# Two column halves for both token tiles of the output projection, with the router's first logits moved into the last block

## The reference, cut to what matters

```
for l in range(DEPTH):
    mix = hybrid_mixer(x, ...)                 # ends in  merged @ w_out
    h = layer_norm(DEEPNORM_ALPHA * x + mix, ln1_g[l], ln1_b[l])
    ffn = hierarchical_moe(h, ...)             # best group of 4, best 2 of its 8 experts
    x = layer_norm(DEEPNORM_ALPHA * h + ffn, ln2_g[l], ln2_b[l])
```

## Time and profile before

| | |
|---|---|
| median of 3 runs | 1603.16 us (1602.19 to 1604.07) |
| the profiled execution, own time | 1602.01 us |
| its span, first to last instruction | 1599.4 us |
| busy: TensorE, VectorE, ScalarE | 81%, 39%, 25% of the span |
| mean granted TensorE clock | 0.903 |
| read from HBM | 522.53 MB, 327 GB/s over the span |

### The profile page before, as it was taken

How to read it: one execution, slowest core, us unless ns; L and a number is a source line. 1 busy time by engine, 2 the same in 40 slices (tenths; PEclk the granted TensorE clock), 3 DMA queues, 4 the chain that set the end, 5 groups by cost and what they waited for, 6 DMA issues and landing times. The chain is left out here.

```text
span 1599.4 us, 21372 instructions
## 1 busy us (share of the span) xinstructions
PE 1298.2 (81%) x8678; PEld 878.4 (55%) x8678; DVE 620.5 (39%) x1063; ACT 393.1 (25%) x453; POOL 0.2 (0%) x4
## 2 busy tenths in 40 slices
PE   9999999999756656657799999999997556656666
PEld 7998889995312212212398988899943212212211
DVE  5788676655100100100287876765641000000102
ACT  4334734323100000001143357343320000000010
POOL 0000000000000000000000000000000000000000
PEclk9999999999978877878999999999999778778778
DMA  8455445689999999999964454376999999999996
GB/s 304 162 194 191 165 158 214 245 356 419 426 428 428 428 427 429 427 427 429 404 223 162 159 211 176 115 257 221 408 420 428 426 426 427 430 426 429 427 425 263
DMA packets 98886, 524.58 MB, mean 328 GB/s; under 512 B 5488, under 2 KB 9968, under 8 KB 70144
## 3 DMA queue, kind: packets, MB, share of 16 engines
q1 hardware_dynamic: 98064, 523.10, 81.2%
q10 hardware_dynamic: 752, 0.50, 0.1%
HBM read 522.53 MB, written 1.05 MB: 327 GB/s over the span
## 5 line engine op out<-in xcount | busy, mean ns | idle before, releaser
L1035 PE MATMUL psum<-ring,aqT 128*32 128x512 f32 x1504 | 269.5, 704 | 112.9 <-PEq L1023 112.9
L1723 DVE TENSOR_TENSOR w_low<-ring,w_high 128x2048 fp32r<-128x2048 f32 (+2 forms) x108 | 239.8, 2260 | 72.3 <-DVEq L1722 71.0
L1281 ACT ACTIVATE w_high<-ring 128x2048 fp32r<-128x2048 f32 (+2 forms) x108 | 198.7, 1887 | 193.3 <-ACTq L1277 178.8
L1035 PE MATMUL psum<-spare,aqT 128*32 128x512 f32 x256 | 130.9, 700 | 94.7 <-PEq L1124 94.7
L1959 DVE TENSOR_TENSOR qk<-psum,qk 128x512 f32<-128x512 f32 x16 | 11.1, 692 | 482.5 <-DVEq L1958 482.5
L1035 PEld LDWEIGHTS psum<-ring,aqT 128*32 128x32 f32 x1504 | 68.6, 127 | 218.1 <-issue 218.1
L1035 PE MATMUL psum<-rv,tmp 128*32 128x512 f32 x240 | 124.2, 707 | 70.0 <-PEq L1151 70.0
L712 PE MATMUL psum<-x_high,w_high 128*128 128x256 f32 x512 | 146.8, 287 | 0.0
L712 PE MATMUL psum<-x_high,w_low 128*128 128x256 f32 x512 | 143.3, 280 | 0.0
L712 PE MATMUL psum<-x_low,w_high 128*128 128x256 f32 x512 | 143.2, 280 | 0.0
L619 PE MATMUL psum<-w_high,x_high 128*128 128x512 f32 (+2 forms) x352 | 138.6, 394 | 0.0
(11 more groups left out here) (266 smaller groups left out, 2280.4 us busy)
## 6 DMA issues: line engine op xcount, KB each, us to landing
ring<-in_w_gate_dram SPq DMA_DIRECT2D x56, 2048.0 KB, 33.0
ring<-in_w_in_dram SPq DMA_DIRECT2D x34, 2048.0 KB, 7.8
ring<-in_w_up_dram SPq DMA_DIRECT2D x28, 2048.0 KB, 21.9
spare<-in_w_up_dram SPq DMA_DIRECT2D x14, 2048.0 KB, 14.2
rv<-in_w_down_dram SPq DMA_DIRECT2D x12, 2048.0 KB, 31.0
rg<-in_w_down_dram SPq DMA_DIRECT2D x12, 2048.0 KB, 35.4
x_xT<-in_w_down_dram SPq DMA_DIRECT2D x12, 2048.0 KB, 39.8
ring<-in_w_down_dram SPq DMA_DIRECT2D x12, 2048.0 KB, 28.9
```

Source lines behind the costliest of these rows:

```text
L1035: mm = nc.tensor.matmul(bank[s, :], lhs[:, c, s], w[:, k, n * NB:(n + 1) * NB], start=(c == 0), stop=(c == chunks - 1))
L1281: nc.scalar.activation(half_tile(high, i % HIGH, w, b), half_tile(ring, i % RAW, w, b), ACT.Copy).then_inc(high_ready, 1)
L1723: V.tensor_tensor(half_tile(low, i % RAW, w, b), half_tile(ring, i % RAW, w, b), half_tile(high, i % HIGH, w, b).bitcast(f32), ALU.subtrac ...
```

## The change

The order of TensorE's work in `out_and_logits` and of VectorE's beside it is changed. The numbers of matmuls, transposes and vector instructions stay the same. The second halves of the sum now run (0,0), (1,0), (0,1), (1,1) left, (1,1) right. The 8 transposes and 8 logits of tile 0 move from the middle of block (1, 0) and ahead of (1,1) left into (1,1) right. VectorE adds up block (1, 0) ahead of (0, 1), and `choose(0)` becomes one piece, ahead of the last `add_up`.

```
                 finish("OUT0", out_block(first[:, 0, :], 0, 0, halves[1], began=out_used[0, 1]))
+                finish("OUT1", out_block(second[:, 0, :], 1, 0, halves[1]))
                 pe.wait_ge(low_ready, 1).then_inc(low_ready, -1)
-                finish("OUT0", out_block(first[:, 1, :], 0, 1, halves[1]))
-                out_block(second[:, 0, :], 1, 0, halves[1][:6])
-
-                pe.wait_ge(y_ready, 2)
+                finish("OUT0", out_block(first[:, 1, :], 0, 1, halves[1], began=out_used[1, 0]))
+                finish("OUT1", out_block(last_left, 1, 1, halves[1], left))
+
+                pe.wait_ge(y_ready, 3)
                 turn_sums(0, range(4), ps[:, 0, :])
                 finish("HT0", turn_sums(0, range(4, KC), first[:, 0, :]))
-                finish("OUT1", out_block(second[:, 0, :], 1, 0, halves[1][6:]))
-
+                out_block(last_right, 1, 1, halves[1][:6], right)
                 rl = begin("RL")
                 copied("HT0", "RL")
-                logits(0, range(KC), rl, began=out_used[1, 0])
-                finish("OUT1", out_block(last_left, 1, 1, halves[1], left))
-
-                out_block(last_right, 1, 1, halves[1][:6], right)
+                logits(0, range(KC), rl)
                 ps = begin("HT1")
-                pe.wait_ge(y_ready, 3)
                 finish("HT1", turn_sums(1, range(4), ps[:, 0, :]))
                 finish("OUT0", out_block(last_right, 1, 1, halves[1][6:], right))
```

```
-                for n in range(2):
-                    c = slice(n * NB, (n + 1) * NB)
-                    add_up(0, c, "OUT0", first[:, n, :])
-                    statistics(0, n, c)
+                add_up(0, slice(0, NB), "OUT0", first[:, 0, :])
+                statistics(0, 0, slice(0, NB))
+                add_up(1, slice(0, NB), "OUT1", second[:, 0, :])
+                statistics(1, 0, quarter[0])
+                statistics(1, 1, quarter[1])
+                add_up(0, slice(NB, 2 * NB), "OUT0", first[:, 1, :])
+                statistics(0, 1, slice(NB, 2 * NB))
...
                 V.tensor_scalar(nmx[:, 2:3], mv[:, 0, 0:1], -1.0, rstd[:, 0:1], ALU.mult, ALU.mult
                                 ).then_inc(norm_ready, 1)
-                add_up(1, slice(0, NB), "OUT1", second[:, 0, :])
-                choose(0, group_found=lambda: statistics(1, 0, quarter[0]),
-                       masked_out=lambda: statistics(1, 1, quarter[1]),
-                       expert_found=lambda: add_up(1, quarter[2], "OUT1",
-                                                   second[:, 1, 0:NB // 2]))
+                add_up(1, quarter[2], "OUT1", second[:, 1, 0:NB // 2])
                 free("OUT1")
                 statistics(1, 2, quarter[2])
+                choose(0)
                 add_up(1, quarter[3], "OUT0", banks("HT0")[:, 1, 0:NB // 2])
```

## The result

The changed kernel takes 1608.67 us (median of 16 runs, 1604.18 to 1612.79), the kernel before 1603.16 (16 runs, 1600.78 to 1604.07). The ratio is 1.0035, 95% interval 1.0029 to 1.0042: **slower by 5.6 us**. The forecast was 3.4 us slower, at most 4.4 by its range. Direction and place were right, the size was not. The profiled execution has 1609.78 us of its own time, 7.8 over the profiled one of before, and a span of 1608.0, 8.6 over it (outside the span lie 1.8 us, before 2.6).

A forecast was written before the change was run, and what follows sets the result against it. The streaming of expert weights bounds the kernel, its queue dry at used(1). A last add_up 1.73 us late costs 1.7 us a layer, 3.4 over two layers, giving 1606.6 us, range 1604.3 to 1607.6.

The forecast's parts named there:

- the place and the mechanism: At used(1) the queue of weight loads is already dry, so a later issue costs its full delay, 1.7 us a layer.
- the term that was summed: Last add_up 1.73 us late, 0.60 from TensorE and 1.13 from its place in VectorE's list; 1.7 us a layer.
- the clock falls: Rival: new TensorE pauses among short matmuls halve the granted clock, 3 us a layer more, in sum +9.4; chance 0.05.
- the 16.11 us of work behind the last add_up: Chain from the last add_up through statistics, choose(1), gather and first gate product to used(1)'s issue, taken as unchanged.
- the second pause: TensorE's wait for sel_ready, from 363.6 to 364.7 us, about 1.1 us.
- nothing in the chain to used(1) has slack, so the 16.11 us stay: From the last add_up to used(1): the delay passes through whole, so used(1) is issued at 380.76 us.
- each later load call finds more queued: After used(1) the queue fills; used(1) alone adds 4 MiB, about 10 us, so the pause there decides.
- The queue hides part: Rival at used(1): loads start quicker behind running transfers, 0.92 us of cover, 0.8 a layer, +1.6; chance 0.22.
- the 0.6 us of first-byte latency: At used(1), by the skill's figure, 0.7 us of queue would be left: 1.0 a layer, sum 2.0.
- the trace's 1.79: Time from a load's issue into an empty queue to its flow, 1.79 us, taken for used(1)'s loads.
- Faster for want of queued work: Rival: two loads issued 4.0 us earlier raise the stream's 414 GB/s, 1.6 us a layer, -3.2; chance 0.05.

The follow-up runs named there:

- the clock held: Changed kernel with 2 unread transposes in TensorE's pause at ScalarE's copies and 4 ahead of sel_ready of tile 0: 1607.2 us, ratio 1.0026.
- the two filled kernels: Changed kernel with unread transposes in the pauses at ScalarE's copies and sel_ready: 1607.2 us, 1.0026; with those at sel_ready only: 1606.19 us, 1.0023.
- kernels with the same used(1): Changed kernel with unread transposes at copies and sel_ready, 1607.2 us; at sel_ready only, 1606.19 us; the latter again, 1607.42 us.
- 0.88 and 0.87 us of lateness: Kernel before with 7 unread transposes instead of 3 ahead of the second gather: 1604.7 us, ratio 1.0011.
- one of 1.52 us behind denser work: Kernel before without its 6 unread transposes between the first gather and the wait for tile 1's sel_ready: 1602.03 us, ratio 0.9995.

## Why the prediction was wrong, and where it was right

**Right: the place and the mechanism.** The stream of weights is all but dry at used(1), and only a few tenths of a us of a delay there are covered. All kernels with a late used(1) are longer, and the changed kernel's flow is behind by nearly the lateness (3.3 and 4.6 us of bytes for 3.33 and 4.99).

**Right: the term that was summed.** The last add_up was forecast 1.73 us late and is 1.71; TensorE's starts agree to 0.03 us. With the clock held, used(1) is 1.71 and 1.74 late and the span +3.3, against +3.4. That the span agrees so closely is partly luck, since the bytes give 1.3 us a layer at used(1) and the later places add to it. The timed runs of the two filled kernels give +4.2 and +3.7 by the ratio.

**Wrong: "the clock falls", given a chance of 0.05.** This is the step that failed: the sum took the 16.11 us of work behind the last add_up at full clock. The rival's mechanism, pauses among short matmuls, is the one that acts, and the second pause was foreseen (1.1, measured 1.23). I set it aside for one row, where TensorE is busy for 0.05 us of 1 us and the clock stays 1.00. That pause brought no fall at all: the clock is 1.00 in every microsecond from 415 to 423 as well. But it stands behind long uninterrupted work (busy for 5.05 of the 6 us from 409 to 415, against 4.22 of 6 up to the end of the changed kernel's pause), so it was no model for a pause among short matmuls. A row of the pause itself could not have shown the fall either way. In the changed kernel it has 1.00 at 364 to 365 and 365 to 366, and 0.50 only from 367. In a much longer pause it is the same (kernel before, second layer, TensorE idle from 1239 on):

```profile
1240.00:1243.00 3.00, 0.00 (x0) 0.00 (x0) 0.00 (x0) 0.00 (x0) 0.00 (x0) 1.00 1.00 426
1243.00:1246.00 3.00, 0.00 (x0) 0.00 (x0) 0.00 (x0) 0.00 (x0) 0.00 (x0) 0.62 1.02 429
1246.00:1249.00 3.00, 0.00 (x0) 0.00 (x0) 0.00 (x0) 0.00 (x0) 0.00 (x0) 0.50 1.00 426
```

The clock answers after its cause, so the rows behind a pause are the ones to read. What I put on the price, 3 us a layer, holds for the second layer (3.25) and is twice what the first pays (1.62). In sum the rival said +9.4; the profiled execution has 3.4 for the order and 1.6 + 3.3 for the clock, 8.3 of lateness and +8.6 of span. The timed median is less, +5.6: the profiled execution of before is itself 1.15 us under its median and that of the changed kernel 1.1 over its own, and probably the clock doesn't fall in every layer of the timed runs (it did in six of the eight profiled).

**Wrong: "nothing in the chain to used(1) has slack, so the 16.11 us stay".** They stay only for VectorE. With the clock down TensorE's own list, gather and unread transposes, becomes the longer way: `sel` is there at 370.00 and is read at 371.76.

**Missing: the places after used(1).** I wrote that each later load call finds more queued, and did not count to the next wait at 447.09, which has 0.5 us in hand by the same count. A late kernel can lose again there, from nothing to some 4 us over both layers. That goes far to explain why kernels with the same used(1) differ in span by 3 us (+3.3, +4.7, +6.2).

**The other rivals.** The queue hides part: refuted in its size, by the bytes missing behind 0.88 and 0.87 us of lateness; a cover of a few tenths is there. By the 0.6 us of first-byte latency that the Trainium skill gives ("DMA: Bandwidth & Descriptors", "Specifications") 0.7 us a layer would have been covered and 1.0 lost, by the trace's 1.79 all of 1.7 lost; the bytes with the clock held say 1.3, between the two. No run here shows a first byte by itself. Faster for want of queued work: the loads that go 4 us earlier (354.18) change nothing, 416 GB/s from 349 to 373 us against 420 before.

**Open.** What the granted clock needs in order to fall. A pause of 1.23 us brought it down in six of eight layers, one of 1.52 us behind denser work in none of two. How often the later places lose, and why the clock falls there in one execution and not in another. Taking the unread transposes out of the changed kernel, which would shorten TensorE's list when the clock is low, was not tried. No version beats the kernel before.

## What to carry to other kernels

Where the end is a stream of transfers, count bytes issued against bytes moved up to every wait of the issuing queue, not only to the first: the one with no margin turns lateness into time nearly one to one. A reordering that brings a new wait of TensorE among light work has a second price besides the wait, the granted clock behind it; look at the microseconds after such a pause, not at the pause, take no pause among other work as its model, and try a few unread matmuls in it. A piece of vector work moved behind another is cheap only if neither of the two paths that meet at the next release gets longer.

## What was not expected of the hardware

- The granted clock fell to half behind a pause of only 1.23 us (sel_ready read at 364.82, clock 0.60 over 366 to 370), and stayed there through 3 us of uninterrupted matmuls in the first layer (367 to 370) and 6 in the second (0.51 over 1162 to 1168). It did not fall behind a pause of 1.52 us.
- The same kernel with the same pause shows the fall in one execution's second layer and not in another's (used(1) 4.99 and 1.75 us late).
- A load issued into an empty queue flowed 1.79 us after its issue (an estimate from the earlier trace rows). The bytes missing behind a late used(1) are somewhat fewer than that implies: 0.64 and 0.48 us for 0.88, 1.3 for 1.7.
